# Rotary and mix chunks as one stage, four-part stores of the rotated halves, and two weight preparations moved earlier

## What is computed

```python
h = rmsnorm(x, norm_pre_g)
z = h @ w_in                      # 2048 x 1024 @ 1024 x 4096
q, k, v, g_attn, c_h, c_b, c_c, g_conv = split(z)   # 768,768,768,768,256,256,256,256
q = rope(q); k = rope(k)          # 12 heads of 64, halves of 32 turned by cos and sin
...                               # three dilated windows of attention over q, k, v, times silu(g_attn)
conv_out = c_b * causal_depthwise_conv(c_c * c_h, conv_w) * silu(g_conv)
y = concat([attn_out, conv_out]) @ w_out
x = x + rmsnorm(y, norm_post_g)
```

## Time and profile before

| | |
|---|---|
| median of 3 runs | 2259.65 us |
| profiled execution | 2263.17 us, span 2261.3 us |
| PE / DVE / ACT / POOL busy | 2024.0 / 1524.7 / 980.3 / 982.8 us |
| share of the last chain | PE 26%, DVE 23%, POOL 11%, DMA 7% |
| mean granted clock of TensorE | 0.957 of full speed |
| norm stage's dense groups end, rope begins | 1136.9 us |
| rope ends on PE, mix's fourth product begins | 1397.5 us, 1420.4 us |
| mix ends on PE, gate's fourth product begins | 1568.8 us, 1573.2 us |

### The profile page before, as it was taken

The page is one execution under the profiler, slowest core; times in us unless marked ns, Lnnn a source line. Parts: engine busy times, 40 slices in busy tenths (PEclk is TensorE's granted clock), DMA queues, the critical chain, the costliest instruction groups (busy, mean ns, idle before and its releaser), DMA issues.

```text
span 2261.3 us, 43932 instructions
## 1 busy us (share of the span) xinstructions
PE 2024.0 (90%) x16552; PEld 1498.2 (66%) x16552; DVE 1524.7 (67%) x3562; ACT 980.3 (43%) x2117; POOL 982.8 (43%) x1064
## 2 busy tenths in 40 slices
PE   5999999996888999698899986899989888787998
PEld 3545868886887887587744433345977777665886
DVE  7615949765996556778656776454399999995422
ACT  4323334222884011332433443233189999882111
POOL 4312333363434998433332231434033888974222
PEclk9999999998999999899999998899999999998999
DMA  5441321346632242422232221122467888674552
GB/s 183 140 118 54 111 73 45 96 145 200 154 91 100 93 154 107 140 95 67 66 103 75 64 86 51 43 75 68 95 137 163 203 201 194 167 207 140 165 172 87
DMA packets 272977, 267.38 MB, mean 118 GB/s; under 512 B 35344, under 2 KB 224656, under 8 KB 272512
## 3 DMA queue, kind: packets, MB, share of 16 engines
q1 hardware_dynamic: 268720, 258.48, 40.2%
q0 software_dynamic: 1680, 5.51, 0.7%
q10 hardware_dynamic: 2368, 0.60, 0.1%
HBM read 171.22 MB, written 93.31 MB: 117 GB/s over the span
## 4 chain that ended last, share of the span: by engine, by line
PE 26%; DVE 23%; POOL 11%; DMA 7%; issue 6%; ACT 3%; SPq 0%; DVEq 0%; ACTq 0%; POOLq 0%
PE bank L445 12%; PE bank L3104 7%; DVE s2m L2953 5%; DVE p2l L2959 4%; PE bank L173 3%; DMA scr_k2l<-qt 2%; DMA scr_q2l<-qt 2%; POOL xr L2008 2%; POOL xr L1995 2%; POOL xr L1993 2%; POOL xr L2010 1%; PE bank L1637 1%; DVE xl L851 1%; DVE qt L2247 1%; DVE qx L2209 1%
## 5 line engine op out<-in xcount | busy, mean ns | idle before, releaser
L173 PE MATMUL bank<-w1h,xh 128*128 128x256 f16 x768 | 210.7, 274 | 3.0 <-DVE s1st L1169 3.0
L173 PE MATMUL bank<-w1l,xh 128*128 128x256 f16 x768 | 210.6, 274 | 0.0
L173 PE MATMUL bank<-w1h,xl 128*128 128x256 f16 x768 | 210.5, 274 | 0.0
L2898 PE MATMUL bank<-ident,p2r 128*128 128x128 f32 x900 | 165.8, 297 | 49.6 <-DVE p2l L2959 42.9
L445 PE MATMUL bank<-xh,w2h 128*128 128x512 f16 x320 | 126.9, 397 | 45.8 <-DVE u L2356 22.9
L2898 PEld LDWEIGHTS bank<-ident,p2r 128*128 128x128 f32 x900 | 97.5, 145 | 106.0 <-DVE p2l L2959 103.3
L2959 DVE SCALAR_TENSOR_TENSOR p2l<-bank,p2h 128x512 f16<-128x512 f32 (+1 forms) x288 | 163.6, 568 | 3.0 <-ACT p2h L2925 2.8
L1179 DVE SCALAR_TENSOR_TENSOR bank<-ain,cw,bank 128x512 f32<-128x512 f32 x208 | 157.0, 755 | 8.0 <-ACT bank L1124 1.7
L2953 DVE CUSTOM_DVE_ANT_0 s2m<-bank,both,finv 128x256 f32<-128x256 f32 (+1 forms) x384 | 160.2, 454 | 0.0
L173 PE MATMUL bank<-w2h,xh 128*128 128x256 f16 x512 | 143.2, 280 | 14.5 <-DVE xl L851 13.5
L2932 ACT ACTIVATE p2r<-s2m,ob 128x128 f32<-128x128 f32 (+1 forms) x384 | 147.5, 436 | 13.1 <-DVE ob L2953 12.7
(11 more groups left out here) (457 smaller groups left out, 6361.1 us busy)
## 6 DMA issues: line engine op xcount, KB each, us to landing
scr_part<-ob SPq DMA_DIRECT2D x48, 264.0 KB, 2.7
cm<-scr_part SPq DMA_DIRECT2D x48, 264.0 KB, 4.6
v<-scr_v SPq DMA_DIRECT2D x192, 65.0 KB, 2.7
ax<-in_x SPq DMA_DIRECT2D x16, 512.0 KB, 5.7
xr<-in_x SPq DMA_DIRECT2D x16, 512.0 KB, 4.5
bx<-scr_x SPq DMA_DIRECT2D x16, 512.0 KB, 7.7
x2r<-scr_x SPq DMA_DIRECT2D x16, 512.0 KB, 4.3
out<-yo SPq DMA_DIRECT2D x16, 512.0 KB, 2.9
```

Of the source, the lines that this page charges most:

```text
L173: ins = nc.tensor.matmul(dst, x, y, start=k == 0 and m == 0, stop=k == n - 1 and m == 2)
L2898: ins = nc.tensor.transpose(bank[:, w * hh + 128 * c:w * hh + 128 * c + 128], p[:, hh, 128 * c:128 * c + 128], ident[:])
```

## The change

1. `rope_stage` and `mix_stage` become `rope_mix_stage`: 20 pairs run through one list, with one PE sequence, and mix's buffers lie in the same SBUF room (`rm`) as those of rope, which it reuses as they come free. The waits on everything at the seam are replaced by waits on single events.
2. Each rotated half is stored by four DMAs of 32 rows instead of one with a three-level destination; the stores of the fp16 high parts are issued by ACT, behind a wait for its own cast; SP issues those of the low parts.
3. In `norm_stage` chunk 3 is squared in four parts too (`spread`), and the squares and totals of chunks 3 and 4 stand earlier in the list.
4. Behind the joined stage ACT and DVE no longer wait for the last stores of the convolution (`c2h`, `c2l`); POOL and SP still do.

```diff
-            work += [("cast", 0, "T2"), ("split", 2), ("pair", 0, "T4"), ("cast", 0, "T4"), ("group", 1, 3), ("tail", 0, "T2"),
-                     ("pair", 0, "T3"), ("cast", 0, "T3"), ("load", 3), ("tail", 0, "T4"), ("group", 2, 1), ("total", 3), ("tail", 0, "T3"),
-                     ("pair", 1, "T1"), ("scaled", 3), ("group", 2, 3), ("pair", 1, "T2"), ("cast", 1, "T2"), ("group", 2, 0), ("load", 4),
-                     ("pair", 1, "T4"), ("cast", 1, "T4"), ("tail", 1, "T2"), ("total", 4), ("group", 2, 2), ("scaled", 4), ("tail", 1, "T4"),
+            work += [("cast", 0, "T2"), ("split", 2), ("load", 3), ("pair", 0, "T4"), ("cast", 0, "T4"), ("group", 1, 3), ("tail", 0, "T2"),
+                     ("pair", 0, "T3"), ("total", 3), ("cast", 0, "T3"), ("tail", 0, "T4"), ("group", 2, 1), ("tail", 0, "T3"), ("scaled", 3),
+                     ("pair", 1, "T1"), ("group", 2, 3), ("load", 4), ("pair", 1, "T2"), ("cast", 1, "T2"), ("group", 2, 0), ("total", 4),
+                     ("pair", 1, "T4"), ("cast", 1, "T4"), ("tail", 1, "T2"), ("group", 2, 2), ("scaled", 4), ("tail", 1, "T4"),
...
+        ROPE, ALL = 12, 20
...
+        room = sb("rm", [128, 10752], scope=scope)
+        cosT, sinT = room[:, 0:2048], room[:, 2048:4096]
+        qx, qt = [room[:, at:at + 1024] for at in (4096, 5120, 6144)], [room[:, at:at + 1024] for at in (7168, 8192)]
+        m1, u2, u4 = ([room[:, at:at + 512], room[:, 512 * k:512 * k + 512]] for k, at in enumerate((9216, 9728, 10240)))
+        uin, acc = room[:, 1536:1536 + S + 2], room[:, 3600:3600 + S]
...
+        stored = [s.at(64 * ROPE) for s in (*h_out, *l_out)]
...
-        def store(i, step, m):
+        def store(queue, i, step, m, done):
             n, P = i // 2, i % 2
-            dst = ((q2h, q2l), (k2h, k2l))[n // 3][m].rearrange("(n h t e) s -> n t h e s", h=4, t=2, e=32)
-            return nc.sync.dma_start(dst[n % 3, step][:, :, 1024 * P:1024 * P + 1024], qt[step][:].bitcast(FH)[:, 1024 * m:1024 * m + 1024])
+            dst, r = ((q2h, q2l), (k2h, k2l))[n // 3][m], 256 * (n % 3) + 32 * step
+            for h in range(4):
+                queue.dma_start(dst[r + 64 * h:r + 64 * h + 32, 1024 * P:1024 * P + 1024],
+                                  qt[step].bitcast(FH)[32 * h:32 * h + 32, 1024 * m:1024 * m + 1024]).then_inc(*done.up(16))
...
                     nc.scalar.activation(half(i, step, 0), whole(i, step), ACT.Copy).then_inc(*a_qh.up())
+                    act.wait_ge(*a_qh.now())
+                    store(nc.scalar, i, step, 0, h_out[step])
...
-                    dve.wait_ge(*h_out[step].at(16 * i))
-                    dve.wait_ge(*l_out[step].at(16 * i))
+                dve.wait_ge(*h_out[step].at(64 * i))
+                dve.wait_ge(*l_out[step].at(64 * i))
...
-    chunks2 += [chunk("n", [(G2, 256)])]
+    chunks2 += [chunk("n", [(G2, 256)], spread=True)]
...
-            rope_stage(s2, wts, 4, xs, xs_ready, fits)
-            wait_all(hand_over())
-        with stack() as s2:
-            mix_stage(s2, wts, 10, xs)
-            wait_all(hand_over())
+            stores = rope_mix_stage(s2, wts, 4, xs, xs_ready, fits)
+            done = hand_over()
+            wait_all(done, (pool, sp))
+            wait_all([x for x in done if x[0] not in stores], (act, dve))
```

More of the change, by code:

```diff
@@ L91, in hand_over, with wait_all @@
         return new
-    def wait_all(new):
-        for eng in (act, dve, pool, sp):
+    def wait_all(new, engines=None):
+        for eng in engines or (act, dve, pool, sp):
             for s, n in new:
@@ L198, in __init__ @@
             done = 0 if first is None else 1
-            by_parts = [c["seven"] for c in chunks]
+            by_parts = [c["spread"] for c in chunks]
             self.summed = [(self.a_n, self.a_n.n + n + 1 - done + 3 * sum(by_parts[:n + 1])) for n in range(len(chunks))]
@@ L272, in pe_total @@
             pe.wait_ge(*before)
-            own, k = (self.parts_[:, n, :], 4) if self.chunks[n]["seven"] else (self.size[:, n, 0:1], 1)
+            own, k = (self.parts_[:, n, :], 4) if self.chunks[n]["spread"] else (self.size[:, n, 0:1], 1)
             nc.tensor.matmul(bank[:, 0:k], ones_[:], own, start=True, stop=True).then_inc(*self.p_t.up())
@@ L552, in norm_stage @@
                 made[item] = d_tl.at(n_tail)
-            elif item[0] == "load" and item[1] > 3:
+            elif item[0] == "load" and item[1] > 2 and late:
                 junk_bank[item[1]] = bk.take(wts.summed[item[1]])
@@ L2092, in slots_of @@
                 work += [(x, *done) for x in outs]
-                for later, what in after(done[1]):
+                for later, what in after(*done):
                     due.setdefault(at + later, []).append((what, *done))
@@ new lines, in dve_rope @@
+        def dve_rope(what, i):
+            c = slice(1024 * (i % 2), 1024 * (i % 2) + 1024)
+            if what in ("cross_low", "cross_high"):
+                step = int(what == "cross_low")
+                if step:
+                    dve.wait_ge(*c_in.at(80))
+                    dve.wait_ge(*a_q.at(i + 1))
+                dve.wait_ge(*d_u.at(5 * i + (4 if step else 5)))
+                dve.wait_ge(*h_out[step].at(64 * i))
+                dve.wait_ge(*l_out[step].at(64 * i))
+                dve_turn(qt[step], (low if step else high)(i), sinT[:, c], ALU.mult)
+            elif what == "high":
+                dve_turn(high(i), high(i), cosT[:, c], ALU.mult)
+                dve_turn(high(i), high(i), qt[1], ALU.add)
+            elif what == "low":
+                dve_turn(low(i), low(i), cosT[:, c], ALU.mult)
+            elif what == "low_add":
+                dve_turn(low(i), low(i), qt[0], ALU.subtract)
+            elif what in ("high_lo", "low_lo"):
+                step = int(what == "high_lo")
+                dve.wait_ge(*a_qh.at(2 * i + 2 - step))
+                nc.vector.tensor_tensor(half(i, step, 1), whole(i, step), half(i, step, 0), ALU.subtract).then_inc(*d_ql.up())
@@ new lines, in dve_conv @@
+        def dve_conv(i, c, P):
+            at, n = 1024 * P, 1024 * P + 1024
+            dve.wait_ge(*mul_at(i, 3))
+            dve.wait_ge(*d_z.now())
+            dve.wait_ge(*REST)
+            dve.wait_ge(*d_ql.at(2 * ROPE))
+            nc.vector.tensor_scalar(acc[:, at:n], uin[:, at:n], cw2[:, c, 0:1], None, ALU.mult).then_inc(*d_cv.up())
+            for m in range(1, 3):
+                dve.wait_ge(*d_cv.now())
+                nc.vector.scalar_tensor_tensor(acc[:, at:n], uin[:, at + m:n + m], cw2[:, c, m:m + 1], acc[:, at:n], ALU.mult, ALU.add).then_inc(*d_cv.up())
@@ new lines, in dve_mix @@
+        def dve_mix(what, i, q):
+            conv, c, P, j = of(i)
+            if conv:
+                if what == "tail" and q == 3:
+                    dve_conv(i, c, P)
+                return
+            if what == "times" and q in (0, 3):
+                b = q // 3
+                dve.wait_ge(*a_th.at(2 * j + 1 + b))
+                nc.vector.scalar_tensor_tensor(tbuf[b], tbuf[b], 1.0, (u4, u2)[b][P], ALU.add, ALU.mult).then_inc(*d_bs.up())
+            if (what, q) in (("tail", 2), ("times", 3)):
+                b = q - 2
+                s = 1024 * P + 512 * (1 - b)
+                if b == 0:
+                    dve.wait_ge(*mul_at(i, 2))
+                dve.wait_ge(*d_bs.now())
+                nc.vector.scalar_tensor_tensor(tbuf[b], tbuf[b], 0.5, acc[:, s:s + 512], ALU.mult, ALU.mult).then_inc(*d_bs.up())
+            if what == "last" and q in (2, 3):
+                b = q - 2
+                dve.wait_ge(*a_bh.at(2 * j + 1 + b))
+                dve.wait_ge(*l2_out[b].at(16 * j))
+                for s in stored:
+                    dve.wait_ge(*s)
+                nc.vector.scalar_tensor_tensor(lbuf[b], tbuf[b], 1.0, f(hbuf[b]), ALU.mult, ALU.subtract).then_inc(*d_bl.up())
@@ L2253, in dve_program @@
                     wts.dve_prep(first + item[1] + 1, item[2])
[L2255 to L2265, removed]
-            nc.sync.dma_start(cosT[:], A["c_cos"]).then_inc(*c_in.up(16))
-            for item in work:
-                if item[0] == "load":
-                    wts.sp_load(first + item[1] + 2)
-                elif item[0] in ("high_hi", "low_hi"):
-                    i, step = item[1], int(item[0] == "high_hi")
-                    sp.wait_ge(*a_qh.at(2 * i + 2 - step))
-                    store(i, step, 0).then_inc(*h_out[step].up(16))
-                elif item[0] in ("high_lo", "low_lo"):
-                    i, step = item[1], int(item[0] == "high_lo")
-                    sp.wait_ge(*d_ql.at(2 * i + 2 - step))
-                    store(i, step, 1).then_inc(*l_out[step].up(16))
@@ L2427, in pool_program @@
+                elif item[0] in ("cross_low", "cross_high", "high", "low", "low_add", "high_lo", "low_lo"):
+                    dve_rope(item[0], item[1])
         def pool_program():
@@ L2446, in sp_program @@
                     wts.sp_load(first + item[1] + 2)
```

(4 more changed lines are left out.)

315 lines of the change are left out of this document (118 added, 197 removed).

## The result

The changed kernel takes **2195.0 us** (median, 2194.0 to 2200.2) where the one before took 2260.0: ratio 0.9717, 95% interval 0.97 to 0.9734. The prediction said 2194.6, in a range of 2176 to 2215. The profiled execution took 2200.2 us, its span 2198.3, where the forecast for that kind of execution was 2198.1. Ahead of everything the change touches it is 2.0 us later than the trace of the kernel before (at the same instruction 1039.93 against 1037.96); behind the gate stage it wins these 2.0 us back. Neither belongs to the change.

A forecast was written before the change was run, and what follows sets the result against it. PE was taken as the bound, losing time in waits and slow-clock stretches: 83.7 us recoverable less 18.6 for new waits gives 65.1, so 2263.2 - 65.1 = 2198.1 profiled; the median, 3.5 lower, 2194.6 us, range 2176 to 2215.

The forecast's parts named there:

- Price of the stalls, norm: Norm stage: two waits for totals of squares, 7.8 and 6.0 us, plus slow clock; all 19.2 us saved, bounds 11 and 19.2.
- Norm's exit: End of the norm stage, before rope: its wait of 1.89 us was to stay.
- Stores: Rope's stores: four DMAs of 32 rows land in 4.0 us against 10.4, so DVE's waits for stores go.
- What is late next: Even pairs of rope and pair 12: POOL meets DVE's products, PE waits 2.4 us; 3.1 each with slow stretch, 18.6 in all.
- the 7.1 us: Pair 4 of rope: DVE's time from corner start to end of `u2`, 12.1 us, less its 5.01 us store wait.
- The slow stretch behind each wait: Behind each remaining even-pair wait in rope and at pair 12: 0.7 us of slow clock, between none and 1.6.
- 38.5 forecast (31.7 + 25.4 - 18.6): Rope's inside stalls 31.7 us plus the rope and mix seam 25.4, less 18.6 for new waits from POOL meetings.
- ACT: ACT's 16 store issues per chunk, 7.2 us on top of 19.3 busy, were costed at nothing.
- The slower rival: ACT becomes rope's bound through its issues, at 1.9 us an issue; 2314 us at 2.5; slower or no change 0.03.
- Mix to gate: Seam of mix and gate: wait of 4.4 us plus 3.0 slow clock, all 7.4 us saved, bounds 4.4 and 7.4.

The follow-up runs named there:

- first kernel of the norm experiment: Changed kernel with the norm stage's last chunks in the old order and chunk 3's square single again: 2220.0 us, ratio 0.9821.
- its second: Changed kernel with the norm stage's last chunks in the old order, but chunk 3's squares still in four parts: 2217.1 us, ratio 0.9811.
- POOL late: Changed kernel with ACT's casts and POOL's low parts of the next weights two slots later in the joined stage, DVE's sums unmoved: 2177.8 us, ratio 0.9634.

## Why the prediction was right, point by point

- **Price of the stalls, norm.** 19.2 forecast, 19.7 in the trace. Right.
- **Norm's exit.** "The exit of this stage keeps its wait of 1.89": wrong, it went, 1.9 us in our favour. PE waited there for DVE's `u2`, behind L379, which stands for the norm stage's last store. From the last L883 to L379 DVE idled 5.04 us before, 4.51 in the first kernel of the norm experiment, and 3.14 in its second and in the changed kernel:

```profile
1123.88 0.69 DVE L379 TENSOR_TENSOR w2s<-w2r 128x512 f32<-128x512 f32 x1 [3.14 <-DMA scr_sg<-bvo]
```

So in these four traces it goes with chunk 3's square in parts, not with the order; by what way the square reaches that store stays open.
- **Stores.** Landing within 4.0 us was assumed; each DMA lands 1.7 to 2.2 us after its issue, four issues by ACT take 1.74, so the last lands after about 3.5 us, an estimate. DVE's waits for them fell to 0.4 us. Right, and the single store and the pair of 64 rows show that it is the slowest dimension of the access pattern, 4 or 2, that sets the share of the DMA engines (0.24 to 0.25, and 0.13). Of the two rules of the Trainium skill weighed in the prediction (DMA: Bandwidth & Descriptors, Rules for kernel authors), the one on the slowest dimension decided; the advice against two transfers to disjoint halves did not apply, since the single transfer never used sixteen engines.
- **What is late next.** A wait of 2.4 us in each even pair was forecast, six of them: 2.35 six times, and the reason is shown by the run that takes POOL away from there. That the length came out so closely is luck, since two parts of the sum were off and made up for each other: meetings of 3.7 us where I had 2.6, and 3.7 - 2.35 leaves DVE 1.4 us of room where I gave it 0.25. One fault stands on both sides. The meeting of 0.83 us at `high`, with the second pair of POOL operations, was already in the 7.1 us that I took from the old trace, in the row of 2.06 us. Without it DVE's queue is 6.3 us (1154.31 to 1160.58 with POOL late), not 7.1. I then used the same 0.83 as the price of the first meeting, which is another one and measured 0.99.
- **The slow stretch behind each wait.** 0.7 us each was chosen between none and 1.6. Five of the six cost 1.7, one nothing, 8.5 in all against 4.2. This is the mis-sized term; it is the difference between 38.5 forecast (31.7 + 25.4 - 18.6) and 34.1 measured for rope with its seam. The entry wait (1.9) and norm (0.5) go the other way, and with 0.3 at the gate 2.3 us too much are left in the sum, less than executions differ by. That the median came within 0.4 us of the forecast is luck too.
- **ACT.** Costed at nothing: right, since a kernel without its issues takes the same time. The slower rival needed 1.9 us an issue; they take 0.44 (1.74 for four).
- **Mix to gate.** 7.4 forecast, 7.1 in the trace, 8.6 when undone.

What the parts are worth, each undone alone, by ratios and medians: norm 21 to 25 us, stores 16 to 18, seam of mix and gate 7 to 9, ACT's issuing 0. The join wasn't undone alone. With stores split and rope and mix apart, the seam still costs a wait of 12.1 us with a slow clock behind it, against 2.4 in the joined stage.

## What to carry over

Ask of a stall not only what it costs but what it covers: behind the store waits lay a meeting of DVE and POOL that cost nothing until the stores were fast, and moving POOL's part by two slots gave another 17 to 19 us. Before moving work behind one deadline, count the queue up to the next one too. Of a slow DMA look at the share of the engines that it keeps busy and at the slowest dimension of its pattern; splitting it helps when each part has a longer one, and hurts badly when it is shorter.

## Unexpected of the hardware

- Two DMAs with a slowest dimension of 2 moved a half's low part in 16.5 to 17.7 us, where one with a dimension of 4 took 7.2 to 9.3 and four of 32 plain rows about 3.5, an estimate. More DMAs under way, on two queues, added nothing there: the share stayed at 0.13.
- The same wait of 2.35 us is followed by 3.4 us at a granted clock of 0.51 in five of six places, and by no slow stretch in one, which lies at another pair in another kernel (pair 4 in the changed one, 1206.59; in the one with SP's stores the fifth). What decides it was not found. Waits of 0.88, of 1.38 (with the norm stage's old order) and of 1.89 us had none. The first matmul behind a wait doesn't tell: it shows 0.39 us at once behind the 2.35 at 1165.98 too, and the slow stretch begins 1.1 us later.
- A DVE operation with two inputs in SBUF, 0.68 us alone, took 2.60 beside POOL's 1024-column subtraction, while the sums with one input in PSUM kept 0.74 to 0.75. The Trainium skill (SBUF — State Buffer, SBUF: two separate sides) says that a DVE instruction with two SBUF inputs and a GpSimd instruction that reads SBUF take a shared pair of ports in turns, each for a whole instruction; these rows agree.
